# Low parts of the z weights, from the fifth block on, made by GpSimd instead of VectorE

## The chip, the cores and the metric

The program runs on one core of one Trainium2 chip. The metric is the device time of one execution in microseconds (us), taken as the median of three runs. The core has a matrix engine (TensorE, PE in the profile), a vector engine (VectorE, DVE), an activation engine (ScalarE, ACT), GpSimd (POOL) and a queue that issues DMAs (SyncE, SP).

## The reference

Three blocks of a network run over 256 tokens of width 1024, in float32. The stage that matters here belongs to the first of them, an RWKV-7 layer that has a convolution branch beside it. Cut to the lines that this stage computes:

```python
proj = h @ w_in[i]                                   # 1024 -> 7168
p_r, p_k, p_v, p_c, z_rwkv, z_conv = jnp.split(proj, splits, axis=-1)
y_rwkv = rwkv7_time_mix(h, p_r, p_k, p_v, ...)       # a recurrence over the tokens
c = u * jax.nn.sigmoid(gate)                         # u, gate = split(p_c)
c = causal_depthwise_conv(c, conv_dw, 31 taps) + dw_b
y_conv = jax.nn.silu(layer_norm(c, ln_w, ln_b)) @ w_o
merged = jax.nn.sigmoid(z_rwkv) * y_rwkv + jax.nn.sigmoid(z_conv) * y_conv
```

## The kernel before, in words

Every large matrix product is made of three products of split float32 values: `w_hi*x_hi + w_hi*x_lo + w_lo*x_hi`. A weight matrix arrives in units of 512 columns in one of two buffers `raw`. A unit is cut in four items of 128 columns. For each item ScalarE copies the raw weights to the rounded `w_hi[m]` (`act_head`, L498) and VectorE makes `w_lo[m] = raw - w_hi[m]`, 128 partitions by 1024 elements (`dve_rest`, L504). SyncE loads the next unit into a buffer half when the `w_lo_ready` count says that its two items have been used.

The layer `z` (the projections z_rwkv and z_conv) is 16 such items, j = 0 to 15, and is not done in a stretch of its own. TensorE spreads its blocks (L2349 to L2351, 24 products of 128x256 each) over the chunk loop of the recurrence. Two blocks come before the loop, and the eight chunks c = 0 to 7 have 2, 2, 2, 2, 1, 1, 1 and 3 blocks (`Z_CHUNK`). The item that block j + 4 will use is prepared once block j is done: ScalarE makes its high part in the same chunk (L1038 and L971), VectorE its low part one chunk later, between the evacuations of z blocks (L1648). Items 4 and 5 are prepared before the loop, in the middle of a triangular inverse that VectorE computes by substitution (L1580 and L1582).

One chunk passes between the engines in this order:

- TensorE: x products (L2435, L2439), eight transposes (L2244), the z blocks, y products (L2449), u products (L2457).
- VectorE and ScalarE: half of the u rows each (VectorE L1721, L1722; "u rows" below).
- VectorE: the state times its decay (L1733, two inputs in SBUF), the masks of the next chunk's products (L1679, two of them, which read PSUM), the state plus the new products (L1688, which reads PSUM). TensorE's x products of the next chunk wait for the masks and for the state.
- VectorE, behind that and in its program order: 12 or 16 taps of the convolution (L1670, 128 by about 240 elements, two inputs in SBUF), then the evacuations of the z blocks and the low parts.

VectorE's instructions are executed in order, so the u rows of a chunk wait for its taps, evacuations and low parts. GpSimd has nothing to do in the loop before chunk 6, where it issues two DMAs (L746).

Of the kernel before, what the change touches and what calls it, by code (L numbers as in the profile page):

```python
# [18 lines left out]
F32 = mybir.dt.float32  # L19
F32R = mybir.dt.float32r  # L20
ALU = mybir.AluOpType
# [3 lines left out]
P = 128  # L25
# [6 lines left out]
M_PER_UNIT = UNIT_COLS // P  # L32
# [47 lines left out]
def build(nc, a, out):  # L80
    ctx = ExitStack()
    with ctx:
        sems = {}

        def sem(name):
            if name not in sems:
                sems[name] = ctx.enter_context(nc.semaphore(name))
            return sems[name]
# [5 lines left out]
        raw = [sb(f"raw{i}", [P, KC, UNIT_COLS]) for i in range(2)]  # L94
        w_hi = [sb(f"w_hi{i}", [P, KC, P], F32R) for i in range(M_PER_UNIT)]
        w_lo = [sb(f"w_lo{i}", [P, KC, P], F32R) for i in range(M_PER_UNIT)]
# [53 lines left out]
        Z_EARLY, Z_CHUNK = 2, (2, 2, 2, 2, 1, 1, 1, 3)  # L150
# [153 lines left out]
        L = {}  # L304
# [32 lines left out]

        landed = [[0, 0], [0, 0]]
        unit, item, evac = 0, 0, 0
        occupant, kept_by_k = [[None, None], [None, None]], [False, False]  # L340
        for ly in order:
            ly.u0, ly.item0, ly.evac0 = unit, item, evac
            ly.landed, ly.free = ([], []), ([], [])
            for u in range(len(ly)):
                s = unit % 2
                for half in range(2):
                    landed[s][half] += 16 * ly.dmas[half]
                    ly.landed[half].append(landed[s][half])
                    ly.free[half].append(occupant[s][1 if ly.by_k != kept_by_k[s] else half])
                    occupant[s][half] = ("w_lo_ready", item + M_PER_UNIT // 2 * (half + 1))  # L350
                    if half:
                        kept_by_k[s] = ly.by_k
                unit += 1
                item += M_PER_UNIT
                if u % ly.k_split == ly.k_split - 1:
                    evac += M_PER_UNIT
            ly.item1, ly.evac1 = item, evac
# [18 lines left out]
        BANKS = M_PER_UNIT  # L376
# [123 lines left out]
        def dve_rest(dve, ly, u, p, m):  # L500
            s = (ly.u0 + p) % 2
            nk = ly.nkc[u] if isinstance(u, int) else KC
            dve.wait_ge(sem("w_hi_ready"), ly.item0 + M_PER_UNIT * u + m + 1)
            dve.tensor_tensor(piece(ly, u, w_lo[m], nk, m), raw_piece(ly, u, s, nk, m), piece(ly, u, w_hi[m], nk, m).bitcast(F32),  # L504
                              ALU.subtract).then_inc(sem("w_lo_ready"), 1)
# [116 lines left out]
        @block.sync  # L622
        def _(sp):
            sp.dma_start(x_tok, a["x"][0].rearrange("(c p) d -> p c d", p=P)).then_inc(sem("x_loaded"), 16)

            load_params(sp, range(1), "par_first", slice(0, PAR_SHARE))
            for ly in order:
                s0 = ly.u0 % 2
                def body(u, p, last):
                    s = (ly.u0 + p) % 2  # L630
                    nk = ly.nkc[u] if isinstance(u, int) else KC
                    for half in range(2):
                        parts = ly.sources(u)[half:half + 1] if ly.by_k else [x for x in ly.sources(u) if x[0].start // HALF == half]
                        if not parts:
                            continue

                        if not isinstance(u, int):
                            sp.wait_ge(sem("w_lo_ready"), ly.item0 + M_PER_UNIT * (u - 2) + M_PER_UNIT // 2 * (half + 1))
                        elif ly.free[half][u]:
                            sp.wait_ge(sem(ly.free[half][u][0]), ly.free[half][u][1])  # L640
                        for c, src in parts:
                            dst = raw[s][:, c, :] if ly.by_k else raw[s][:, 0:nk, c]
                            sp.dma_start(dst, src).then_inc(sem(f"landed{s}{half}"), 16)
                if ly.name == "down0":
                    sp.wait_ge(sem("w_lo_ready"), L["up0"].item1)
                    sp.dma_start(dt_w, a["ssd_w_in_2"][0].rearrange("(k p) n -> p k n", p=P)[:, :, 5120:5120 + SSD_HEADS]).then_inc(sem("dt_w_loaded"), 16)
                if ly.name == "down1":
                    sp.wait_ge(sem("w_lo_ready"), L["up1"].item1)
                    sp.dma_start(fox_w, a["fox_w_in_2"][0].rearrange("(k p) n -> p k n", p=P)[:, :, 4 * D:4 * D + FOX_HEADS]).then_inc(sem("small_loaded"), 16)
                if ly.name == "down2":  # L650
                    sp.dma_start(gain_last, a["final_norm_g_2"].rearrange("(a d) -> a d", a=1).broadcast_to([P, D])).then_inc(sem("small_loaded"), 16)
                if ly.name == "conv_out":
                    for i, name in enumerate(("ssd_dt_bias_2", "ssd_a_log_2")):
                        sp.dma_start(heads_col[:, i:i + 1], a[name][0].rearrange("(h a) -> h a", a=1)).then_inc(sem("small_loaded"), 16)
                    sp.dma_start(heads_col[0:FOX_HEADS, 2:3], a["fox_b_f_2"][0].rearrange("(h a) -> h a", a=1)).then_inc(sem("small_loaded"), 16)
                    for h in range(2):
                        for i, name in enumerate(("fox_q_norm_g_2", "fox_k_norm_g_2")):
                            sp.dma_start(fox_g[64 * h:64 * h + 64, i:i + 1], a[name][0].rearrange("(d a) -> d a", a=1)).then_inc(sem("small_loaded"), 16)
                        sp.dma_start(d_rows[64 * h:64 * h + 64, :], a["ssd_d_2"][0].rearrange("(a h) -> a h", a=1).broadcast_to([64, SSD_HEADS])).then_inc(sem("small_loaded"), 16)
                if ly is order[0]:  # L660
                    for u in range(len(ly)):
                        if u == 2:

                            load_params(sp, range(1, par_tiles), "par_loaded")
                        body(u, u % 2, False)
                    for i, (n, rows) in enumerate((("decay_w2", slice(0, 64)), ("a_2", slice(64, 128)), ("g_2", slice(0, 128)))):
                        sp.dma_start(w2[rows, D * i:D * i + D], a[n][0]).then_inc(sem("small_loaded"), 16)
                else:
                    units(sp, ly, body)
            for i in range(4):  # L670
                c, b = divmod(i, 2)
                half = slice(UNIT_COLS * b, UNIT_COLS * b + UNIT_COLS)
                sp.wait_ge(sem(f"y_tok_ready{b}"), c + 1)
                sp.dma_start(out[0, c * P:(c + 1) * P, half], y_tok[:, c, half]).then_inc(sem("out_done"), 16)
            sp.wait_ge(sem("out_done"), 64)
# [3 lines left out]
        def _(pool):  # L679
# [55 lines left out]
            for r in range(4):  # L735
                pool.dma_start(lt[quarter[r]], sub_in[quarter[r]].rearrange("s (y t) -> y s t", t=CHUNK)).then_inc(sem("sub_dma"), 16)

            pool.wait_ge(sem("dve_stages"), INVERSES_MADE)
            link(pool.memset(state, 0.0))
            pool.nop().then_inc(sem("pool_stages"), 1)  # L740

            pool.wait_ge(sem("bonus_out"), 16)
            pool.wait_ge(sem("ln_act"), 2)
# [674 lines left out]
        def _(dve):  # L1418
# [212 lines left out]
                    substitute(done, done + SUB_STEPS[i - SUB_BLOCK])  # L1631

            def z_rest(j):
                dve_rest(dve, L["z"], j // M_PER_UNIT, j // M_PER_UNIT % 2, j % M_PER_UNIT)

            def z_rests(first, last):
# [270 lines left out]
            ly = L["ssd_xbc"]  # L1907
# [192 lines left out]
            ly = L["fox_v"]  # L2100
# [113 lines left out]
        def _(pe):  # L2214
# [122 lines left out]
            def z_blocks(first, last, c=None):  # L2337

                ly = L["z"]
                for j in range(first, min(last, len(ly) * M_PER_UNIT)):  # L2340
                    m = j % M_PER_UNIT
                    if j % 2 and c is not None:
                        pe.wait_ge(sem("x_rows_a"), c + 1)
                    pe.wait_ge(sem("w_lo_ready"), ly.item0 + j + 1)
                    if j >= 2:

                        pe.wait_ge(sem("evac_done"), ly.evac0 + BANKS + j - 1)
                    for k in range(KC):
                        mm(z_bank(j), w_hi[m][:, k, :], x_hi[:, k, :], start=k == 0, stop=False)  # L2349
                        mm(z_bank(j), w_hi[m][:, k, :], x_lo[:, k, :], start=False, stop=False)  # L2350
                        ins = mm(z_bank(j), w_lo[m][:, k, :], x_hi[:, k, :], start=False, stop=k == KC - 1)  # L2351
                    ins.then_inc(sem("block_done"), 1)
# [409 lines left out]
```

## Time and profile before

| | us |
|---|---|
| median of three runs | 1379.92 |
| lowest and highest | 1376.66, 1382.22 |
| the profiled execution | 1387.18 |
| its span in the trace | 1385.4 |

The profiled execution is 7.3 us above the median. Its span is 1.8 us shorter than its own time. Time stamps of rows are in us from the start of the span. In a timeline row stand the start, the duration, the engine, the line, the operation with its output and inputs, how many instructions of one kind were merged, and in brackets the idle time of the engine before it and what ended it. A duration of one instruction includes the time from its start to its end on the engine, and two that follow each other overlap by about 0.1 us.

### The profile page before, as it was taken

The page shows a single profiled execution, that of the slowest core. Times are in us where ns is not written, and L with a number is a line of the kernel's source. Part 1 is how long each engine was busy: PE and PEld are TensorE (multiplying, and loading weights), DVE is VectorE, ACT ScalarE, POOL GpSimd, SP SyncE. Part 2 cuts the span into 40 slices and gives each one's busy share as a digit, 9 for nine tenths or more (in the row PEclk, how much of TensorE's full clock was granted, in tenths as well). Part 3 has the DMA queues.
Part 4 walks back from the last instruction along what each step waited for, and adds up shares of the span by engine and source line. Part 5 has one row for each costly group of instructions (what it writes and reads, how often), then busy time and mean ns, then how long its engine had stood idle before and what let it go on. Part 6 is the DMA issues. An engine that isn't in the chain of part 4 may idle for free.

```text
span 1385.4 us, 30051 instructions
## 1 busy us (share of the span) xinstructions
PE 1329.5 (96%) x12384; PEld 1267.8 (92%) x12384; DVE 992.7 (72%) x1636; ACT 774.7 (56%) x1353; POOL 116.5 (8%) x151
## 2 busy tenths in 40 slices
PE   5999999999999999999997999999999999999998
PEld 5998978989989999989995899999999888999986
DVE  4769898978876665575898868886565554877754
ACT  4596775549455443454669654444455554644443
POOL 2000100000002110000203001111000100122100
PEclk8999998999999999999999999999999998999999
DMA  7643620223545537645672355546664621555461
GB/s 226 195 140 123 191 86 27 70 68 118 183 153 183 183 122 232 189 132 182 199 213 75 121 175 164 183 150 208 190 183 166 196 65 57 188 183 182 163 212 66
DMA packets 197810, 212.70 MB, mean 154 GB/s; under 512 B 8972, under 2 KB 186924, under 8 KB 197564
## 3 DMA queue, kind: packets, MB, share of 16 engines
q1 hardware_dynamic: 195132, 201.46, 45.4%
q0 software_dynamic: 2464, 9.52, 2.3%
q8 instruction: 89, 1.46, 0.4%
q14 instruction: 29, 0.24, 0.1%
q10 hardware_dynamic: 96, 0.02, 0.0%
HBM read 209.33 MB, written 1.65 MB: 152 GB/s over the span
## 4 chain that ended last, share of the span: by engine, by line
PE 88%; DVE 6%; ACT 2%; SPq 2%; issue 1%; DMA 1%; DVEq 0%; ACTq 0%
PE pb L458 21%; PE pb L459 21%; PE pb L460 21%; PE pb L2405 2%; PE pb L2729 1%; PE pb L2730 1%; PE pb L2731 1%; PE pb L2244 1%; PE pb L2233 1%; SPq L610 1%; DVE w_lo L504 1%; PE pb L2349 1%; PE pb L2350 1%; PE pb L2351 1%; DVE pj L1670 1%
## 5 line engine op out<-in xcount | busy, mean ns | idle before, releaser
L504 DVE TENSOR_TENSOR w_lo<-raw,w_hi 128x1024 fp32r<-128x1024 f32 (+2 forms) x384 | 465.6, 1216 | 139.6 <-ACT w_hi L498 138.4
L498 ACT ACTIVATE w_hi<-raw 128x1024 fp32r<-128x1024 f32 (+2 forms) x384 | 396.6, 1041 | 301.1 <-PE pb L460 221.4
L458 PE MATMUL pb<-x_hi,w_hi 128*128 128x256 f32 x1856 | 529.6, 285 | 5.9 <-DVE x_lo L1427 3.5
L459 PE MATMUL pb<-x_lo,w_hi 128*128 128x256 f32 x1856 | 527.1, 284 | 0.0
L460 PE MATMUL pb<-x_hi,w_lo 128*128 128x256 f32 x1856 | 526.9, 284 | 0.0
L458 PEld LDWEIGHTS pb<-x_hi,w_hi 128*128 128x128 f32 x1856 | 358.2, 193 | 8.8 <-DVE w_lo L504 6.7
L459 PEld LDWEIGHTS pb<-x_lo,w_hi 128*128 128x128 f32 x1856 | 358.3, 193 | 0.2
L460 PEld LDWEIGHTS pb<-x_hi,w_lo 128*128 128x128 f32 x1856 | 358.2, 193 | 0.0
L753 POOL TENSOR_TENSOR sub<-sub,rstd 128x256 f32<-128x256 f32 x66 | 72.0, 1106 | 584.1 <-ACT sub L1146 584.1
L458 PE MATMUL pb<-act_hi,w_hi 128*128 128x256 f32 x392 | 111.1, 284 | 3.3 <-DVE w_lo L504 3.3
L460 PE MATMUL pb<-act_hi,w_lo 128*128 128x256 f32 x392 | 110.9, 283 | 0.0
L459 PE MATMUL pb<-act_lo,w_hi 128*128 128x256 f32 x352 | 99.6, 283 | 0.0
L1146 ACT ACTIVATE sub<-sub 128x256 f32<-128x256 f32 x66 | 26.5, 415 | 100.7 <-DVE sub L1875 84.0
L458 PEld LDWEIGHTS pb<-act_hi,w_hi 128*128 128x128 f32 x392 | 75.2, 192 | 3.7 <-DVE w_lo L504 3.7
L460 PEld LDWEIGHTS pb<-act_hi,w_lo 128*128 128x128 f32 x392 | 75.3, 192 | 0.0
L459 PEld LDWEIGHTS pb<-act_lo,w_hi 128*128 128x128 f32 x352 | 67.6, 192 | 0.0
L1846 DVE TENSOR_TENSOR sub<-pb,rstd 128x256 f32<-128x256 f32 x66 | 27.8, 423 | 45.3 <-PE pb L460 42.6
L1852 DVE TENSOR_TENSOR sub<-pb,sub 128x256 f32<-128x256 f32 x66 | 27.7, 420 | 40.1 <-PE pb L460 22.2
L1153 ACT ACTIVATE act_hi<-sub 128x256 f32 (+1 forms) x66 | 27.3, 416 | 45.5 <-DVE sub L1852 45.5
L1670 DVE SCALAR_TENSOR_TENSOR pj<-pj,par 128x255 f32<-128x255 f32 (+29 forms) x120 | 48.3, 464 | 0.9
L1444 DVE TENSOR_TENSOR pj<-pb,rstd 128x256 f32<-128x256 f32 x64 | 26.9, 422 | 25.3 <-PE pb L460 24.0
L2244 PE MATMUL pb<-ident,pj 128*128 128x128 f32 (+1 forms) x195 | 34.9, 323 | 9.4 <-DMA pj<-in_x_dram 6.0
(363 smaller groups left out, 2277.1 us busy)
## 6 DMA issues: line engine op xcount, KB each, us to landing
raw<-in_ffn_w_up_dram SPq DMA_DIRECT2D x55, 1024.0 KB, 5.1
raw<-in_w_in_dram SPq DMA_DIRECT2D x28, 1024.0 KB, 5.1
raw<-in_ssd_w_in_dram SPq DMA_DIRECT2D x20, 1024.0 KB, 5.3
raw<-in_ffn_w_down_dram SPq DMA_DIRECT2D x16, 1024.0 KB, 5.6
raw<-in_fox_w_in_dram SPq DMA_DIRECT2D x16, 1024.0 KB, 5.8
raw<-in_ffn_w_down_dram SPq DMA_DIRECT2D x16, 896.0 KB, 5.8
raw<-in_ffn_w_gate_dram SPq DMA_DIRECT2D x11, 1024.0 KB, 5.3
raw<-in_ssd_w_out_dram SPq DMA_DIRECT2D x8, 1024.0 KB, 5.2
```

The costliest lines, as they stand in the source:

```text
L458: pe.matmul(o, w_hi[m][:, k, :], hi[:, k0 + k, :], start=first and k == 0, stop=False)
L459: pe.matmul(o, w_hi[m][:, k, :], lo[:, k0 + k, :], start=False, stop=False)
L460: mm = pe.matmul(o, w_lo[m][:, k, :], hi[:, k0 + k, :], start=False, stop=final and k == nk - 1)
L498: act.activation(piece(ly, u, w_hi[m], nk, m), raw_piece(ly, u, s, nk, m), ACT.Copy).then_inc(sem("w_hi_ready"), 1)
L504: dve.tensor_tensor(piece(ly, u, w_lo[m], nk, m), raw_piece(ly, u, s, nk, m), piece(ly, u, w_hi[m], nk, m).bitcast(F32), ALU.subtract).the ...
L753: pool.tensor_tensor(s_tile[m], s_tile[m], rstd[:, :], ALU.mult).then_inc(sem("glu_silu"), 1)
L1153: act.activation(o, a_tile[m], ACT.Copy).then_inc(sem("act_hi_ready"), 1)
L1670: go(stt(o[:, s:T], c[:, 0:T - s], w, o[:, s:T], ALU.mult, ALU.add))
L1846: tt(g_tile[m], pb[m][:, 0:T], rstd[:, :], ALU.mult).then_inc(sem("evac_done"), 1)
L1852: tt(a_tile[m - 2], pb[m][:, 0:T], s_tile[m - 2], ALU.mult).then_inc(sem("evac_done"), 1)
L2244: return pe.transpose(o, i, ident[0:n, 0:n])
L2405: ins = mm(pb[PAIR_BANKS[q][a]][side[c], s:T], diag[(2 * i + c) % NDIAG][side[a], :], slot(U)[side[a], 2 * q + c, 0:T - s], start=s == 0, ...
```

## The change

GpSimd subtracts the high parts for items 4 to 15 of the layer `z`, in a new function `z_low` that waits for the high part (`w_hi_ready`) and counts in a semaphore of its own, `low_z`. It makes items 4 and 5 before it waits for the inverse (L739 before), and the other ten behind it, ahead of its two DMAs of the bonus term. Where VectorE made these 12 low parts there now stands a nop that only raises `w_lo_ready`. TensorE waits for `low_z` as well before z block j, and so does SyncE before it refills a half of `raw` that these items occupied.

```diff
+        POOL_LOW = {}
+        POOL_LOW["z"] = lambda u, last: M_PER_UNIT * (u - 1) + last
...
                             sp.wait_ge(sem(ly.free[half][u][0]), ly.free[half][u][1])
+                            if ly.free[half][u][3] > 0:
+                                sp.wait_ge(sem(f"low_{ly.free[half][u][2]}"), ly.free[half][u][3])
...
+            def z_low(j):
+
+                ly, m = L["z"], j % M_PER_UNIT
+                s = (ly.u0 + j // M_PER_UNIT) % 2
+                pool.wait_ge(sem("w_hi_ready"), ly.item0 + j + 1)
+                pool.tensor_tensor(w_lo[m][:, :, :], raw[s][:, :, P * m:P * m + P], w_hi[m][:, :, :].bitcast(F32),
+                                   ALU.subtract).then_inc(sem("low_z"), 1)
+            for j in range(BANKS, BANKS + Z_EARLY):
+                z_low(j)
             pool.wait_ge(sem("dve_stages"), INVERSES_MADE)
             link(pool.memset(state, 0.0))
             pool.nop().then_inc(sem("pool_stages"), 1)
+            for j in range(BANKS + Z_EARLY, len(L["z"]) * M_PER_UNIT):
+                z_low(j)
...
             def z_rest(j):
+                if j >= BANKS:
+
+                    dve.nop().then_inc(sem("w_lo_ready"), 1)
+                    return
                 dve_rest(dve, L["z"], j // M_PER_UNIT, j // M_PER_UNIT % 2, j % M_PER_UNIT)
...
                     pe.wait_ge(sem("w_lo_ready"), ly.item0 + j + 1)
+                    if j >= BANKS:
+                        pe.wait_ge(sem("low_z"), j - BANKS + 1)
```

VectorE at the end of chunk 1, before the change: the last taps, the two evacuations with the low parts of items 6 and 7, the u rows, the decayed state and the masks.

```order
L1670 SCALAR_TENSOR_TENSOR pj<-pj,par 128x242 x3
L1648 TENSOR_TENSOR pj<-pb,rstd 128x256 [waits block_done,dve_chain]
L504 TENSOR_TENSOR w_lo<-raw,w_hi 128x1024 [waits w_hi_ready]
L1648 TENSOR_TENSOR pj<-pb,rstd 128x256 [waits block_done]
L504 TENSOR_TENSOR w_lo<-raw,w_hi 128x1024 [waits w_hi_ready]
L1721 COPY pj<-pb 32x2x128 [waits u_done]
L1722 COPY pj<-pb 32x2x128
L1733 TENSOR_TENSOR sub<-sub,chunk_decay 128x512 [waits y1_done]
```

The same place after the change (lines of the changed kernel: L1668 is the evacuation, L1741 and L1742 the u rows, L1753 the decayed state).

```order
L1690 SCALAR_TENSOR_TENSOR pj<-pj,par 128x242 x3
L1668 TENSOR_TENSOR pj<-pb,rstd 128x256 [waits block_done,dve_chain]
L1668 TENSOR_TENSOR pj<-pb,rstd 128x256 [waits block_done]
L1741 COPY pj<-pb 32x2x128 [waits u_done]
L1742 COPY pj<-pb 32x2x128
L1753 TENSOR_TENSOR sub<-sub,chunk_decay 128x512 [waits y1_done]
```

The two subtractions have left VectorE's queue between the evacuations and the u rows; nothing else has moved.

GpSimd from its loads for the inverse to the DMAs of the bonus, before the change.

```order
L736 DMA sub<-sub_in 32x32x32 x3
L739 MEMSET sub 128x512 [waits dve_stages]
L746 DMA pj<-bonus_dram 64x8x256 [waits pool_chain,ln_act,bonus_out]
L746 DMA pj<-bonus_dram 64x8x256
```

The same place after the change (L748 is the subtraction in `z_low`, L753 the memset of the state, L762 the DMAs).

```order
L741 DMA sub<-sub_in 32x32x32 x3
L748 TENSOR_TENSOR w_lo<-raw,w_hi 128x1024 [waits w_hi_ready] x2
L753 MEMSET sub 128x512 [waits dve_stages]
L748 TENSOR_TENSOR w_lo<-raw,w_hi 128x1024 [waits pool_chain,w_hi_ready]
L748 TENSOR_TENSOR w_lo<-raw,w_hi 128x1024 [waits w_hi_ready] x9
L762 DMA pj<-bonus_dram 64x8x256 [waits ln_act,bonus_out]
```

Twelve subtractions now stand on GpSimd, two ahead of the memset and ten between it and the DMAs.

## Rows read from the trace of the kernel before

**Rows 1.** The page, busy time of each engine

```profile
PE 1329.5 (96%) x12384; PEld 1267.8 (92%) x12384; DVE 992.7 (72%) x1636; ACT 774.7 (56%) x1353; POOL 116.5 (8%) x151
```

**Rows 2.** Timeline of VectorE and TensorE: substitution, and its first user

```profile
189.26 2.36 DVE L504 TENSOR_TENSOR w_lo<-raw,w_hi 128x1024 fp32r<-128x1024 f32 x2
...
206.21 3.54 PE L2416 MATMUL pb<-ident,sub 32*32 32x32 f32 x233
```

**Rows 3.** Timeline of VectorE, early taps to the u rows of chunk 0

```profile
203.37 18.50 DVE L1670 SCALAR_TENSOR_TENSOR pj<-pj,par 128x255 f32<-128x255 f32 x44
...
222.76 0.42 DVE L1648 TENSOR_TENSOR pj<-pb,rstd 128x256 f32<-128x256 f32 x1 [0.44 <-PE pb L2351]
224.47 0.41 DVE L1721 COPY pj<-pb 32x256 f32<-32x256 f32 x1 [1.29 <-PE pb L2457]
```

**Rows 4.** Timeline of VectorE, chunks 1 and 2

```profile
239.75 0.69 DVE L1733 TENSOR_TENSOR sub<-sub,chunk_decay 128x512 f32<-128x512 f32 x1
...
242.60 6.52 DVE L1670 SCALAR_TENSOR_TENSOR pj<-pj,par 128x241 f32<-128x241 f32 x16
...
252.21 0.41 DVE L1721 COPY pj<-pb 32x256 f32<-32x256 f32 x1
...
253.10 0.69 DVE L1733 TENSOR_TENSOR sub<-sub,chunk_decay 128x512 f32<-128x512 f32 x1
```

**Rows 5.** Timeline of VectorE, chunks 4 and 5

```profile
276.95 2.35 DVE L504 TENSOR_TENSOR w_lo<-raw,w_hi 128x1024 fp32r<-128x1024 f32 x2
...
280.23 0.69 DVE L1733 TENSOR_TENSOR sub<-sub,chunk_decay 128x512 f32<-128x512 f32 x1
...
296.53 0.69 DVE L1688 TENSOR_TENSOR sub<-sub,pb 128x512 f32<-128x512 f32 x1 [2.48 <-PE pb L2478]
```

**Rows 6.** Timeline of TensorE, u products of chunks 2 and 4

```profile
250.91 0.69 PE L2457 MATMUL pb<-pj 32*32 32x64 f32 x32
...
276.28 0.69 PE L2457 MATMUL pb<-pj 32*32 32x64 f32 x32
```

**Rows 7.** Timeline of ScalarE, high parts of items 6, 7, 9, 10, 11, 14

```profile
219.94 1.06 ACT L498 ACTIVATE w_hi<-raw 128x1024 fp32r<-128x1024 f32 x1 [0.92 <-PE pb L2351]
222.76 1.06 ACT L498 ACTIVATE w_hi<-raw 128x1024 fp32r<-128x1024 f32 x1 [1.75 <-PE pb L2351]
...
237.14 1.06 ACT L498 ACTIVATE w_hi<-raw 128x1024 fp32r<-128x1024 f32 x1 [1.75 <-PE pb L2351]
...
247.26 1.05 ACT L498 ACTIVATE w_hi<-raw 128x1024 fp32r<-128x1024 f32 x1
249.97 1.06 ACT L498 ACTIVATE w_hi<-raw 128x1024 fp32r<-128x1024 f32 x1 [1.67 <-PE pb L2351]
...
275.49 1.04 ACT L498 ACTIVATE w_hi<-raw 128x1024 fp32r<-128x1024 f32 x1
```

**Rows 8.** Instructions of two lines of GpSimd: min/median/max ns

```profile
L753 POOL TENSOR_TENSOR sub<-sub,rstd x66: 727/752/1612, 419.7 to 1317.8; 128x256 f32<-128x256 f32 x66
L719 POOL TENSOR_TENSOR sub<-sub x3: 1269/1294/1525, 17.9 to 20.9; 128x512 f32<-128x512 f32 x3
```

**Rows 9.** Timelines of GpSimd and VectorE where the two meet

```profile
425.51 2.23 POOL L753 TENSOR_TENSOR sub<-sub,rstd 128x256 f32<-128x256 f32 x2 [4.33 <-ACT sub L1146]
...
436.08 1.20 POOL L753 TENSOR_TENSOR sub<-sub,rstd 128x256 f32<-128x256 f32 x1 [1.66 <-ACT sub L1146]
...
427.48 1.34 DVE L504 TENSOR_TENSOR w_lo<-raw,w_hi 128x1024 fp32r<-128x1024 f32 x1
...
435.47 1.22 DVE L504 TENSOR_TENSOR w_lo<-raw,w_hi 128x1024 fp32r<-128x1024 f32 x1
```

**Rows 10.** Eight transposes before the z blocks, chunks 2 and 3

```profile
243.12 1.06 PE L2244 MATMUL pb<-ident,pj 128*64 128x128 f32 x8
...
256.70 1.91 PE L2244 MATMUL pb<-ident,pj 128*64 128x128 f32 x8
```

**Rows 11.** Window of chunk 3: busy time per engine, clock, DMA share, GB/s

```profile
256.00:259.00 3.00, 2.93 (x44) 2.49 (x44) 2.96 (x9) 0.80 (x3) 0.00 (x0) 0.50 0.21 68
```

More of the change, by code:

```diff
@@ L349, in build @@
                     ly.free[half].append(occupant[s][1 if ly.by_k != kept_by_k[s] else half])
-                    occupant[s][half] = ("w_lo_ready", item + M_PER_UNIT // 2 * (half + 1))
+                    last = M_PER_UNIT // 2 * (half + 1)
+                    occupant[s][half] = ("w_lo_ready", item + last, ly.name, POOL_LOW[ly.name](u, last) if ly.name in POOL_LOW else 0)
                     if half:
```

## The prediction

> **What bounds the kernel now.** I read the busy times first [rows 1]: TensorE is busy for 96% of the span, VectorE for 72%, GpSimd for 8%. A change of VectorE's load therefore counts only where TensorE waits for VectorE. The chain that ended last, followed through the stretch from 175 to 330 us, passes to VectorE in one recurring place: at a chunk's end through the u rows, the decayed state L1733, the masks L1679 and the state sum L1688, and from there to TensorE's x products of the next chunk. So I read VectorE's timeline chunk by chunk and asked of every u-rows row whether VectorE had been idle before it. In chunk 0 it was idle for 1.29 us, and for 0.44 us one instruction earlier [rows 3]. In chunk 2 it was not: the u rows start at 252.21 [rows 4], but TensorE's products for them had ended at 250.91 + 0.69 = 251.60 [rows 6]. In chunk 4 TensorE was done at 276.97 [rows 6], and VectorE was still in two low parts from 276.95 on [rows 5]. Those two places are where the 12 subtractions cost time today.
>
> **What is removed.** Twelve subtractions, two in 2.36 us [rows 2], so 14.1 us of VectorE's work. Items 4 and 5 lie in the substitution, whose result TensorE first uses at 206.21 [rows 2], about six us after it is done: worth nothing by themselves. In chunks 1 and 3 VectorE waits for TensorE behind them, in chunks 5 and 6 TensorE's sums of the layer norm are the longer part (VectorE idles for 2.48 us before L1688 of chunk 5 [rows 5]): nothing either. Chunk 2 has 252.21 - 251.60 = 0.6 us to give, chunk 4 has 279.3 - 276.97 = 2.4 us (the low parts start at 276.95 and take 2.35 [rows 5]). The removal alone is worth 3.0 us.
>
> **What one subtraction takes on GpSimd.** Before, GpSimd has no operation of 128x1024. Its two-input operation on 256 elements takes 0.727 us at least and on 512 takes 1.269 us [rows 8], so 256 more elements cost 0.542 us. Going on by that step, 1024 elements take 1.269 + 2 x 0.542 = 2.35 us; four times the 256-element median of 0.752 us gives 3.0 us. I call the value p and take 2.35 us, because the step comes from the largest sizes that the trace has, and keep 2.35 and 3.0 as its bounds. A cheaper one I exclude: the two sizes show no gain per element that would bring it below. The page "GPSIMD Engine Reference" of the Trainium skill, section 3.1, gives 4497 ns for 2048 float32 elements; half of that is an estimate of 2.25 us, with which the sum below would be 3.6 instead of 4.2. No low part is late by this: item 6 is ready some 20 us before its block in chunk 2.
>
> **What it does to VectorE.** The trace shows the two engines in each other's way when both read two inputs from SBUF. GpSimd's instruction at 436.08 starts while VectorE's subtraction of 435.47 to 436.69 runs and takes 1.20 us instead of 0.75 [rows 8, 9]; it ends 0.59 us after VectorE does. The other way round, GpSimd's pair that starts at 425.51 ends at 427.74; VectorE's subtraction that starts at 427.48 takes 1.34 us instead of 1.22, and ends 1.08 us after GpSimd's end [rows 9]. The one that starts second seems to wait for the first. These overlaps of VectorE are short, 0.26 us at most, so that a stall over a whole GpSimd instruction isn't shown by rows, only extrapolated.
>
> The page "SBUF — State Buffer" of the Trainium skill, section "Who interferes with whom", states it as a rule: VectorE with two SBUF inputs and GpSimd reading SBUF share a read port, and the later one blocks fully until the first is done, while a VectorE instruction with one SBUF input doesn't contend. By that rule the sum is the 4.2 us below; without it, 3.0 us would be gained. The trace agrees as far as its short overlaps go.
>
> VectorE's instructions with two SBUF inputs are here the taps L1670 and the decayed state L1733. The evacuations, u rows, masks and the state sum take an operand from PSUM; that GpSimd doesn't hold them is an assumption. So I lay each subtraction at the end of its high part [rows 7] and ask what it meets:
>
> - Items 4 and 5, in the substitution: two stalls of at most 2 x 2.35 = 4.7 us against 2.36 us removed, with reductions of one input running underneath. VectorE ends between 0 and 2.3 us later; I take 0.4. TensorE has six us here, but the early taps, which end at 221.87 [rows 3], then end at about 222.2.
> - Chunk 0: item 6 asks at 219.94 + 1.06 = 221.00, gets in behind a tap at about 221.4 and holds until 223.75. Two taps of 0.4 us are left. One runs; item 7, which asks at 223.82, gets in at 224.15 and holds until 226.5. Then the last tap 0.4 and two evacuations 0.8: the u rows start at 221.4 + 2p + 1.6 = 227.7 instead of 224.47 [rows 3]. Cost 2p - 1.5 = **+3.2**.
> - Chunk 1: item 9 asks at 238.20 and holds until 240.55; L1733 is due at 239.75 [rows 4]. Cost p - 1.55 = **+0.8**. Item 8 meets only evacuations. Nothing hides the delay, as x products follow the masks at once.
> - Chunk 2: item 10 asks at 248.31, in the last taps, which end at 249.12 [rows 4]; with the stall they end at 251.45 and the evacuations at 252.25, where the u rows stood before (252.21). The 0.6 us that were to be gained are gone. Item 11 asks at 251.03, gets in at 251.4 and holds until 253.75; L1733 was at 253.10. Cost p - 1.7 = **+0.65**.
> - Chunk 3 repeats chunk 1, with the same distance of 1.55 us: **+0.8**.
> - Chunk 4: item 14 asks at 276.53, as the taps end, and holds until 278.95. The u rows, no longer held up, are done by 277.9, so L1733 starts at 278.95 instead of 280.23 [rows 5]. Cost p - 3.63 = **-1.3**.
> - Chunk 5: item 15 delays L1733 by half a us, under the 2.48 us that VectorE idles behind it. Nothing. The bonus DMAs on GpSimd's queue, now behind ten subtractions, go out at 309.75 us, long after item 15. Nothing. The extra nops and waits: under 0.1 us each, hidden with their engines' other work.
>
> The sum is 6p - 9.9, with p = 2.35 **+4.2 us**.
>
> One more term is TensorE's clock. In chunk 3 the granted clock is 0.50, the lower of its two levels (1.2 GHz), at the transposes and the first z products [rows 11]; the eight transposes take 1.91 us, against 1.06 in chunk 2 [rows 10], and with the products around them a chunk loses about 1.4 us. Before, chunks 1, 3 and 5 are hit and 2 and 4 not. The small products ahead of the transposes are stretched by the 0.8 us of chunks 1 and 3, which makes that more likely in 2 and 4. It would cost 1.1 us in chunk 2 and 1.3 in chunk 4, where the gain would go. I count half of both, **+1.2 us**.
>
> Together +5.4 us, on the profiled execution's 1387.18 us 1392.6 (span 1385.4 to 1390.8). That execution is above the median of the three runs, 1379.92 us, from which the forecast starts: **1385.3 us**.
>
> **The rivals.**
>
> - *The engines don't block each other for long.* VectorE would then merely lose its 12 subtractions: -3.0 us, 1377 us. For it: the trace has no long stall of VectorE by GpSimd. Against it: both rows above [rows 9], and that every overlap in them costs. Chance 0.13.
> - *A subtraction costs GpSimd 3.0 us or more* (its raw operand is eight pieces of 128 elements, which no operation before has). The sum is 6 x 3.0 - 9.9 = +8.1, with the clock's 1.2 +9.3: 1389.2 us. From p = 2.8 the sum alone is over 6.9 us, which is 0.5%. For it: items 6 and 7, which stall the taps of chunk 0, count twice. Against it: the step between the two sizes measured. A clock that falls in both chunks brings p = 2.35 to +6.6, just short of that bound. Chance of this side 0.28.
> - *The low part comes late and TensorE waits for `low_z`.* It would have to be late by 20 us; chance 0.02 or less, in which the time would be over 1390.
>
> **How the numbers follow.** The forecast, a stall of a few us in the loop, has 0.57. The range reaches from the first rival to past the second: 1376.5 to 1391 us; the likeliest case's own range is 1382 to 1388. Within 0.5% (6.9 us, about what a measurement of this kernel can tell from no change) lie the forecast and the first rival; the chances are 0.03 faster, 0.69 same, 0.28 slower.
>
> **What the changed profile would show.** GpSimd's 12 rows at 2.4 us where VectorE is in evacuations, and longer where it starts in a tap. Single taps, or L1733 of chunks 1 to 3, longer by up to 2.4 us, with the idle time gone. The u rows of chunk 0 some 3 us later, and L1733 of chunk 4 relatively earlier. If taps keep their 0.4 us while GpSimd works, the blocking is wrong and with it the sign. If GpSimd's rows are over 2.8 us outside of the taps, p is.

## The result and the profile after

The changed kernel takes 1393.74 us (median of six runs, 1388.46 to 1396.41), the kernel before 1380.77 us in the same six comparisons: ratio 1.0089, 95% interval 1.0069 to 1.0109, so about 12.3 us slower (9.5 to 15.1). The forecast was 1385.3 us with a range up to 1391.0: the direction was the likeliest case's, the size was not. Two runs stand outside of all means and ratios below, one of 1448.98 us of the kernel before, at a mean granted clock of 0.84, and one of 3255.26 us of experiment e11.

The page after, head and busy times (as in [rows 1]):

```profile
span 1391.4 us, 30074 instructions
PE 1329.5 (96%) x12384; PEld 1268.6 (91%) x12384; DVE 991.5 (71%) x1624; ACT 774.3 (56%) x1353; POOL 145.3 (10%) x163
```

VectorE has lost 12 instructions and only 1.2 us of busy time, where 14.1 us of work were taken away. The difference is in instructions that last longer. The 12 subtractions on GpSimd, with their least, median and greatest duration in ns:

```profile
L748 POOL TENSOR_TENSOR w_lo<-raw,w_hi x12: 2353/2383/3340, 181.4 to 300.6; 128x1024 fp32r<-128x1024 f32 x12
```

GpSimd's timeline (L748 is the subtraction):

```profile
181.39 5.67 POOL L748 TENSOR_TENSOR w_lo<-raw,w_hi 128x1024 fp32r<-128x1024 f32 x2 [34.63 <-ACT w_hi L501]
...
219.41 2.45 POOL L748 TENSOR_TENSOR w_lo<-raw,w_hi 128x1024 fp32r<-128x1024 f32 x1 [17.46 <-ACT w_hi L501]
222.22 2.51 POOL L748 TENSOR_TENSOR w_lo<-raw,w_hi 128x1024 fp32r<-128x1024 f32 x1 [0.36 <-ACT w_hi L501]
...
243.17 2.37 POOL L748 TENSOR_TENSOR w_lo<-raw,w_hi 128x1024 fp32r<-128x1024 f32 x1 [0.42 <-ACT w_hi L501]
...
284.11 2.44 POOL L748 TENSOR_TENSOR w_lo<-raw,w_hi 128x1024 fp32r<-128x1024 f32 x1 [8.48 <-ACT w_hi L501]
```

VectorE in the same stretches (L1596 substitution; L1635 the gated product; L1690 taps; L1741 u rows; L1753 decayed state):

```profile
182.44 2.39 DVE L1635 TENSOR_TENSOR pj<-pj 128x1024 f32<-128x1024 f32 x1
...
185.65 2.79 DVE L1596 TENSOR_TENSOR sub<-sub 128x768 f32<-128x768 f32 x1
...
195.91 1.52 DVE L1596 TENSOR_TENSOR sub<-sub 128x768 f32<-128x768 f32 x1
...
204.44 22.61 DVE L1690 SCALAR_TENSOR_TENSOR pj<-pj,par 128x255 f32<-128x255 f32 x44
...
227.88 0.41 DVE L1741 COPY pj<-pb 32x256 f32<-32x256 f32 x1
...
244.65 1.44 DVE L1753 TENSOR_TENSOR sub<-sub,chunk_decay 128x512 f32<-128x512 f32 x1
...
258.72 1.43 DVE L1753 TENSOR_TENSOR sub<-sub,chunk_decay 128x512 f32<-128x512 f32 x1
...
278.34 8.47 DVE L1690 SCALAR_TENSOR_TENSOR pj<-pj,par 128x233 f32<-128x233 f32 x16
...
287.30 0.41 DVE L1741 COPY pj<-pb 32x256 f32<-32x256 f32 x1
```

A substitution step of 768 elements takes 2.79 us beside GpSimd's subtraction and 1.52 us ten microseconds later, without it. The 44 early taps take 22.61 us instead of 18.50 [rows 3]; the decayed state of chunks 1 and 2 takes 1.44 and 1.43 us instead of 0.69 [rows 4]; the train of 16 taps in which GpSimd starts at 284.11 takes 8.47 us, and the two trains of 16 before it, undisturbed or nearly, take 6.46 and 6.51 us. TensorE waits for what comes behind:

```profile
228.79 1.97 PE L2500 MATMUL pb<-pj,sub 64*64 64x64 f32 x32 [5.00 <-DVE pj L1742]
230.56 1.86 PE L2504 MATMUL pb<-pj 64*64 64x32 f32 x32
...
288.22 1.97 PE L2500 MATMUL pb<-pj,sub 64*64 64x64 f32 x32 [2.68 <-DVE pj L1742]
```

The same batches in chunks 0 and 4 of the kernel before:

```profile
225.38 1.15 PE L2478 MATMUL pb<-pj,sub 64*64 64x64 f32 x32
226.37 1.07 PE L2482 MATMUL pb<-pj 64*64 64x32 f32 x32
...
280.25 1.15 PE L2478 MATMUL pb<-pj,sub 64*64 64x64 f32 x32 [2.20 <-DVE pj L1722]
```

So TensorE has five microseconds of idle time in chunk 0, where before there was none, and 2.68 in chunk 4, where there were 2.20. And the batches of small products are slower behind the wait: 1.97 and 1.86 us instead of 1.15 and 1.07. The windows with the granted clock (columns: the stretch, its length, PE, PEld, DVE, ACT and POOL busy, clock, DMA share, GB/s) show why:

```profile
228.00:240.00 12.00, 11.21 (x169) 10.52 (x170) 8.59 (x19) 4.59 (x14) 0.00 (x0) 0.64 0.01 3
291.00:301.00 10.00, 10.00 (x176) 9.09 (x174) 6.69 (x18) 3.42 (x7) 0.39 (x1) 0.65 0.04 13
321.50:328.50 7.00, 7.00 (x78) 6.86 (x58) 1.24 (x2) 6.70 (x14) 0.06 (x1) 0.53 0.67 152
```

A mean of 0.64 over 12 us is the lower level (1.2 GHz) for most of them; before, the stretches at the lower level, at the start of chunk 0 and in chunks 1, 3 and 5, are a few microseconds each [rows 11]. From the first x product of chunk 0 to the u products of chunk 7 the loop took 318.14 - 212.32 = 105.8 us before and 331.56 - 211.02 = 120.5 us after. By chunk, from one x product's start to the next (us; "filler" is the run e9 below, "delay" e10):

| chunk | 0 | 1 | 2 | 3 | 4 | 5 | 6 | 7 (to u) | sum |
|---|---|---|---|---|---|---|---|---|---|
| before | 15.22 | 14.40 | 13.35 | 15.07 | 12.05 | 15.29 | 12.44 | 8.00 | 105.8 |
| after | 21.33 | 15.22 | 14.07 | 16.15 | 13.99 | 16.35 | 12.44 | 10.99 | 120.5 |
| filler | 19.50 | 13.57 | 13.60 | 13.70 | 12.41 | 14.35 | 12.45 | 7.99 | 107.6 |
| delay | 23.61 | 14.81 | 13.35 | 15.16 | 13.44 | 16.35 | 12.45 | 10.97 | 120.1 |

The loop's 14.7 us are more than the spans' 6.0 us, because the profiled execution of the kernel before is 6 to 7 us slower than its median (part of it a stretch from 1148 to 1178 us with a mean clock of 0.83, against 1.00 in the one after); the medians, 13 us apart, fit the loop.

The whole loop as one window, first before, then after:

```profile
212.32:318.83 106.51, 102.71 (x2097) 94.75 (x2097) 86.62 (x171) 58.64 (x132) 1.38 (x2) 0.92 0.21 62
211.02:332.25 121.23, 110.45 (x2097) 102.24 (x2097) 86.76 (x166) 60.30 (x136) 25.46 (x12) 0.85 0.19 55
```

TensorE is idle for 10.8 us instead of 3.8, and busy for 7.7 us longer with the same 2097 products. In these two executions the loss is thus about half waiting and half the lower clock (36 us at the lower level instead of 17).

### The profile page after: what moved, and what is told of

Same layout as the page of the kernel before. It is cut to its first block, busy times and chain, and to the rows that moved or that the text cites. A ratio compares the mean times of both kernels' runs of the same rounds, so it can differ in the third digit from the quotient of the medians.

```text
span 1391.4 us, 30074 instructions
## 1 busy us (share of the span) xinstructions
PE 1329.5 (96%) x12384; PEld 1268.6 (91%) x12384; DVE 991.5 (71%) x1624; ACT 774.3 (56%) x1353; POOL 145.3 (10%) x163
## 4 chain that ended last, share of the span: by engine, by line
PE 80%; DVE 11%; ACT 3%; DMA 2%; SPq 2%; issue 2%; POOL 0%; DVEq 0%; ACTq 0%; POOLq 0%
PE pb L461 20%; PE pb L463 19%; PE pb L462 19%; DVE pj L1690 2%; DVE w_lo L507 2%; PE pb L2752 1%; PE pb L2753 1%; PE pb L2751 1%; PE pb L2253 1%; SPq L613 1%; PE pb L2264 1%; PE pb L2371 1%; PE pb L2372 1%; PE pb L2373 1%; ACT pj L1298 1%
## 5 line engine op out<-in xcount | busy, mean ns | idle before, releaser
L507 DVE TENSOR_TENSOR w_lo<-raw,w_hi 128x1024 fp32r<-128x1024 f32 (+1 forms) x372 | 451.2, 1216 | 139.6 <-ACT w_hi L501 138.7
L1690 DVE SCALAR_TENSOR_TENSOR pj<-pj,par 128x255 f32<-128x255 f32 (+29 forms) x120 | 54.5, 516 | 0.9
```

Of the source, the lines that this page charges most:

```text
L1690: go(stt(o[:, s:T], c[:, 0:T - s], w, o[:, s:T], ALU.mult, ALU.add))
```

## The experiments

Each kernel was timed beside the kernel before, and every ratio is to that one. "Loop" is the sum of the table above (105.8 us before), taken from the profiled execution.

### e1, the removal alone

```diff
+        POOL_ITEMS = ()
+        POOL_LOW["z"] = lambda u, last: sum(j < M_PER_UNIT * u + last for j in POOL_ITEMS)
...
-            for j in range(BANKS + Z_EARLY, len(L["z"]) * M_PER_UNIT):
+            for j in [j for j in POOL_ITEMS if j >= BANKS + Z_EARLY]:
                 z_low(j)
...
             def z_rest(j):
                 if j >= BANKS:
-
+                    dve.wait_ge(sem("w_hi_ready"), L["z"].item0 + j + 1)
                     dve.nop().then_inc(sem("w_lo_ready"), 1)
```

(The list of items on GpSimd is empty here. The loop for items 4 and 5 and TensorE's wait for `low_z` go by the same list.)

> The 12 low parts are left out altogether (w_lo of items 4 to 15 holds older values), VectorE only waits for the high part and raises the count, GpSimd does nothing for them. This is the removal without its replacement. Theory A (GpSimd's subtractions block VectorE through SBUF, everything else is a consequence): 3.0 us faster than before, the chunk loop (first x product of chunk 0 to the last y product of chunk 7, 109.5 us before, 124.2 after the change) at 106 to 108 us, a ratio near 0.998. Rival B (the loss comes from VectorE's altered order or from the clock that falls when VectorE runs ahead of TensorE, not from GpSimd): as slow as the changed kernel, ratio 1.005 to 1.010, loop over 118 us.

Measured: ratio 0.9996 (0.9979 to 1.0013). Rival B, an effect of VectorE's order alone, is out: nothing is lost. But the 3.0 us of gain don't show either (the interval just reaches 0.998). In the profiled execution the loop is 108.0 us; by the expectation's own measure, which reaches to the last y product, it is 111.7 us against 109.5 before, where 106 to 108 were expected. The gain is where it was forecast, chunk 4 takes 9.77 us instead of 12.05, but chunks 2 and 3 take 16.74 and 18.07 instead of 13.35 and 15.07. There TensorE stops twice in the middle of a batch of small products, at places where no engine released it:

```profile
242.11 0.47 PE L2462 MATMUL pb<-sub,pj 64*32 64x64 f32 x15 [1.15 <-issue]
...
258.66 0.65 PE L2458 MATMUL pb<-pj 32*32 32x64 f32 x11 [1.52 <-issue]
```

The window behind the first, with the clock in the third column from the right:

```profile
242.00:248.00 6.00, 5.89 (x42) 5.44 (x43) 4.89 (x13) 3.54 (x12) 0.00 (x0) 0.52 0.02 4
```

TensorE is at the lower clock there. What VectorE gives back in this execution, TensorE loses in gaps and clock. Over all 12 runs, though, the time at the lower clock is the same as before (41 us in both), so the clock isn't shown to be what takes the gain in the mean. Why the gaps are there and not in the kernel before wasn't found.

### e2, GpSimd writes but doesn't read

On top of e1:

```diff
+            pool.wait_ge(sem("inverse_rows"), CHUNK // INV_GROUP)
+            for j in range(BANKS + Z_EARLY, len(L["z"]) * M_PER_UNIT):
+                pool.wait_ge(sem("w_hi_ready"), L["z"].item0 + j + 1)
+                link(pool.memset(flat_sub[:, 1024:2048], 0.0))
+                link(pool.memset(flat_sub[:, 1024:2048], 0.0))
+                link(pool.memset(flat_sub[:, 1024:1536], 0.0))
```

> As the one before, the 12 low parts left out, but GpSimd runs three memsets (1024, 1024 and 512 elements, some 2.5 us in all) into unused memory at each of the ten places behind the inverse where the changed kernel subtracts (items 6 to 15). They write and read nothing. Theory A in the form that only GpSimd instructions that read SBUF hold VectorE's second operand: VectorE's taps and decayed states keep their 0.4 and 0.69 us, time as without the memsets, ratio 0.996 to 1.000. If any GpSimd instruction holds VectorE: taps stalled as after the change, ratio 1.005 or more. Rival B as for the run without memsets.

Measured: 0.9994 (0.9977 to 1.0012). GpSimd and VectorE in chunk 0:

```profile
224.15 0.95 POOL L760 MEMSET sub<- 128x1024 f32 x1
...
224.57 0.69 DVE L1758 TENSOR_TENSOR sub<-sub,chunk_decay 128x512 f32<-128x512 f32 x1
```

The decayed state runs wholly inside a memset and keeps its 0.69 us. It does so in chunks 1 to 3 too, where it runs beside two memsets each. GpSimd being busy and writing SBUF at the same places isn't what holds VectorE. That its reads are is what is left; no run has an instruction that only reads.

### e3, the two items that should meet nothing

```diff
+        POOL_ITEMS = (8, 12)
...
             def z_rest(j):
-                if j >= BANKS:
+                if j in POOL_ITEMS:
```

and likewise in `z_low`'s loops, in TensorE's wait and in SyncE's counts. The next four experiments differ in this tuple alone.

> GpSimd makes the low parts of items 8 and 12 only; VectorE makes the ten others as before. By the model of stalls those two begin behind the taps of chunks 1 and 3 and end before the decayed state, so they meet no two-input instruction, and their removal shortens VectorE's way to the u rows of chunk 2 by 0.6 us and of chunk 4 by 1.2 us. Theory A: 1.8 us faster than before, ratio 0.997 to 1.001. Rival B (any hand-over to GpSimd costs 1 us an item): 2 us slower, ratio over 1.001.

Measured: 0.9993 (0.9970 to 1.0015), loop 105.0 us. The expected gain of 1.8 us is too small to be told from nothing, and the interval doesn't quite exclude the rival either. In the trace the decayed state has 0.69 us in all chunks. But item 12 does meet something: it starts 0.75 us before the train of taps in chunk 3 would have ended, holds it for 2.1 us (8.57 instead of 6.45), and TensorE gets a wait that the kernel before hasn't:

```profile
255.36 8.57 DVE L1691 SCALAR_TENSOR_TENSOR pj<-pj,par 128x237 f32<-128x237 f32 x16
...
261.06 2.61 POOL L749 TENSOR_TENSOR w_lo<-raw,w_hi 128x1024 fp32r<-128x1024 f32 x1 [23.40 <-ACT w_hi L502]
...
267.94 1.23 PE L2501 MATMUL pb<-pj,sub 64*64 64x64 f32 x32 [1.47 <-DVE pj L1743]
```

In return the wait of 2.20 us in chunk 4 is gone altogether. Item 12 met nothing in the changed kernel (the train of chunk 3 has 6.46 us there): whether an item collides depends on the rest of the loop.

### e4, e5, e6, e7: which items cost

> GpSimd makes items 4 to 7 only, the ones that meet the substitution and the early taps; VectorE makes items 8 to 15 as before. Theory A: this carries the loss of chunk 0, which in the profile of the changed kernel is 6.1 of the 14.7 us by which the loop grew; so 5 to 6 us slower than before, ratio 1.003 to 1.005, with u rows of chunk 0 some 3 to 5 us late and the clock down behind them. If the loss is spread over the loop in proportion to the items (4 of 12): 4.3 us, ratio 1.003, without a stall of over 2 us in chunk 0.

> GpSimd makes items 6 and 7 only, whose two subtractions meet the last early taps of chunk 0; 4 and 5 stay with VectorE, so the substitution is not held. Theory A: the taps end about 4.7 us later than their own length allows (two subtractions of 2.4 us), minus 1 us that the substitution no longer loses; the u rows of chunk 0 come 2 to 4 us late, the whole is 3 to 6 us slower than before, ratio 1.002 to 1.004. Rival C (the substitution's hold by items 4 and 5 is what makes chunk 0 late): no loss, ratio under 1.001.

> GpSimd makes items 4, 5 and 8 to 15; VectorE makes 6 and 7 as before. Theory A: chunk 0 is as before (item 4 and 5 cost the substitution 1 us, of which TensorE waits nothing), and what is left is the decayed state held in chunks 1, 2 and 3 (+0.8, +0.7, +0.8) and item 14 in the taps of chunk 4 (0 to +1.9): 2 to 4 us slower than before, ratio 1.001 to 1.003, and the first wait of TensorE for u rows is short (before: none). Rival (the loss is made by the ten late items together): ratio over 1.005.

> GpSimd makes only the three items whose subtraction meets the decayed state (9, 11, 13). Theory A: the row of the decayed state is 1.4 us instead of 0.69 in chunks 1, 2 and 3, +0.7 us each, against which one low part less stands before the u rows of chunk 2 (-0.6) and of chunk 4 (-1.2): 0 to 1 us slower, ratio 1.000 to 1.002, and no tap longer than 0.5 us.

| items on GpSimd | ratio (95% interval) | loop, us | TensorE's wait in chunk 0, us |
|---|---|---|---|
| 4 to 7 | 1.0063 (1.0044 to 1.0081) | 116.5 | 5.23 |
| 6, 7 | 1.0048 (1.0029 to 1.0068) | 114.0 | 3.94 |
| 4, 5, 8 to 15 | 1.0038 (1.0016 to 1.0060) | 114.1 | 0.52 |
| 9, 11, 13 | 1.0007 (0.9983 to 1.0031) | 107.9 | none |
| all twelve | 1.0089 (1.0069 to 1.0109) | 120.5 | 5.00 |

Items 4 to 7 cost 8.7 us, more than the 5 to 6 expected (their profiled execution is 8 us above their median). Two items of twelve, 6 and 7, make 6.6 us of the 12.3, somewhat more than the 3 to 6 expected. The rest makes 5.2 us, more than the 2 to 4 us expected; the rival's 1.005 lies inside the interval. The two ratios add up to the whole (0.0048 + 0.0038 = 0.0086), each known to about 3 us. In the third kernel the wait in chunk 0 is short, and yet the loop is at a mean clock of 0.87, against 0.92 before: a long wait in chunk 0 isn't needed for the clock to fall more often. Items 9, 11 and 13 hold the decayed state as forecast, in the kernel with these three alone:

```profile
237.44 1.72 DVE L1754 TENSOR_TENSOR sub<-sub,chunk_decay 128x512 f32<-128x512 f32 x1
252.62 1.43 DVE L1754 TENSOR_TENSOR sub<-sub,chunk_decay 128x512 f32<-128x512 f32 x1
268.30 1.42 DVE L1754 TENSOR_TENSOR sub<-sub,chunk_decay 128x512 f32<-128x512 f32 x1
```

and cost 1.0 us (-2.3 to +4.3), since each also removes a low part. Items 4 and 5 alone weren't run; by difference of the first two rows of the table they cost 2 us beside 6 and 7, less than the intervals can resolve.

### e8 and e9, the changed kernel with its idle time filled

```diff
                 else:
                     z_blocks(Z_FIRST[c] + 2, Z_FIRST[c + 1], c)
+                for _ in range({0: 36, 4: 18}.get(c, 0)):
+                    mm(pb[7][:, T:2 * T], x_hi[:, 0, 0:P], x_hi[:, 0, :], start=False, stop=False, skip_group_check=True)
```

(e8 had `start=True, stop=True`; that also changed the y sums, which are added up in the other half of the bank. e9 leaves them alone.)

> The changed kernel, with TensorE given products whose result nobody reads (36 of 128x256 in chunk 0 and 18 in chunk 4, 0.12 us each at full clock, into an unused half of a PSUM bank) just before it waits for the u rows, where it stands idle for 5.0 and 2.7 us in the changed kernel. If the idle time lets the granted clock fall and the lower clock behind it is part of the loss: the clock stays at 1.00 through chunk 1, the products behind the wait take 1.15 and 1.07 us instead of 1.97 and 1.86, and the kernel is 3 to 5 us faster than the changed one: ratio to before 1.005 to 1.007 instead of 1.009. If the clock plays no part: 1.009 as without the filler, or above.

> The changed kernel with the same idle-time products on TensorE as in the run before (36 in chunk 0, 18 in chunk 4), but added onto what stands in the unused half of the bank instead of starting a new sum there, because the first form also disturbed the y sums in the other half of that bank. Theory A (stalls of VectorE some 6 us, lower clock behind them some 8 us): the same time as with the first filler, ratio 1.002 to 1.004, loop from the first x product to the last u product 107 to 109 us (120.5 in the changed kernel, 105.8 before), no low-clock stretch behind chunk 0. Rival (the first filler was fast because the y values it left were different): ratio 1.007 to 1.009.

Measured: 1.0031 (1.0010 to 1.0051) and 1.0048 (1.0030 to 1.0067); the loop of the profiled execution is 107.6 us in both. The first is faster than the 1.005 to 1.007 expected, the second just slower than its 1.002 to 1.004, and both intervals exclude the 1.009 of no effect. All GpSimd subtractions are still there, and VectorE is held for no less in sum, though partly elsewhere: the 44 early taps take 22.63 us in e9, the trains of chunks 2 and 3 are held now and that of chunk 4 no longer:

```profile
244.68 8.66 DVE L1690 SCALAR_TENSOR_TENSOR pj<-pj,par 128x241 f32<-128x241 f32 x16
...
258.28 8.59 DVE L1690 SCALAR_TENSOR_TENSOR pj<-pj,par 128x237 f32<-128x237 f32 x16
...
271.87 6.39 DVE L1690 SCALAR_TENSOR_TENSOR pj<-pj,par 128x233 f32<-128x233 f32 x16
```

TensorE in chunk 0 of e9:

```profile
222.97 4.58 PE L2487 MATMUL pb<-x_hi 128*128 128x256 f32 x36
228.28 1.15 PE L2502 MATMUL pb<-pj,sub 64*64 64x64 f32 x32 [0.73 <-DVE pj L1742]
229.26 1.07 PE L2506 MATMUL pb<-pj 64*64 64x32 f32 x32
```

The window of e9 that answers to 228 to 240 us above:

```profile
222.00:234.00 12.00, 11.04 (x217) 10.43 (x218) 11.55 (x23) 3.92 (x11) 1.83 (x1) 1.00 0.01 3
```

Needless work on the busiest engine makes the kernel faster, by the difference of 1.0089 and the mean of the two, 1.0040, that is 6.8 us, give or take 3.4 by the intervals: about half of the loss was TensorE running at its lower clock behind a wait for VectorE. The rival of e9, that the first filler's y values mattered, is out, as its 1.007 lies above the interval. Both profiled executions are the fastest of their kernels (1379.10 and 1378.68 us, medians 1385.40 and 1387.38), with 14 to 17 us at the lower clock where the mean is 35 and 39. So the row "filler" above shows the loop at its best, not in the mean.

### e10, VectorE late without GpSimd

```diff
             conv_taps(0, DVE_EARLY)
+            dve.wait_ge(sem("inverse_rows"), CHUNK // INV_GROUP)
+            for _ in range(6):
+                link(tt(flat_sub[:, 1024:2048], flat_sub[:, 1024:2048], flat_sub[:, 1024:2048], ALU.subtract))
```

> The kernel before, with nothing on GpSimd, in which VectorE does six needless subtractions of 128x1024 (1.22 us each, 7 us in all) in dead memory at the end of the early taps. By the slack of 1.7 us there the u rows of chunk 0 come 5.2 us late, as in the changed kernel, and no later chunk is touched. Theory A (a long wait costs its length and then the lower clock behind it): TensorE waits 5 us and low-clock stretches follow in chunk 1; the loop grows by 7 to 10 us, ratio 1.005 to 1.008. Rival D (the lower clock in the changed kernel comes from the later collisions, not from the wait in chunk 0): the loop grows by 5.2 us, ratio 1.004.

Measured: 1.0068 (1.0048 to 1.0088). VectorE is held for 7.5 us and TensorE waits longer than planned (timelines of VectorE and TensorE):

```profile
222.21 7.52 DVE L1696 TENSOR_TENSOR sub<-sub 128x1024 f32<-128x1024 f32 x6
...
231.47 1.97 PE L2481 MATMUL pb<-pj,sub 64*64 64x64 f32 x32 [7.93 <-DVE pj L1725]
233.23 1.86 PE L2485 MATMUL pb<-pj 64*64 64x32 f32 x32
```

The window of e10 behind it:

```profile
231.00:243.00 12.00, 11.53 (x169) 10.84 (x170) 8.63 (x19) 4.59 (x14) 0.00 (x0) 0.62 0.01 3
```

The wait came out longer than the 5.2 us expected: the u rows are ready 6.1 us later than before, and TensorE's products ahead of them were done 1.9 us earlier in this execution. The ratio alone doesn't separate theory A from rival D, since the wait of 7.9 us by itself would be 1.0057, inside the interval. The trace does: rows and clock behind the wait are those of the changed kernel (1.97 and 1.86 us, 0.62), and in the loop TensorE is busy for 109.5 us instead of 102.7 with the same products. In the table above its chunks 5 and 7 are as long as the changed kernel's to 0.02 us, with no GpSimd instruction in them. So the longer chunks 5 and 7 after the change aren't collisions. Chunk 7 begins at 320.6 us in both and falls to the lower clock; what decides that, the runs don't show.

### e11 and e12, filler where it might pay

Kernel before with 18 such products in its wait in chunk 4, and items 8 and 12 on GpSimd with 12 of them.

> The kernel before with 18 needless products of 128x256 on TensorE in its wait of 2.2 us in chunk 4, added onto an unused half bank. If the clock is worth having: the low-clock stretch of chunk 5 (283.0 to 287.0) is gone, 1 to 2 us faster than before, ratio 0.998 to 1.000; if not, the same time, or 0.3 us slower as the products outlast the wait.

> GpSimd makes items 8 and 12 only, and TensorE does 12 needless products in its wait of 1.5 us in chunk 4, where the run with items 8 and 12 alone has 6.8 us at the lower clock behind it. Theory A: the gains of both, loop 102 to 104 us instead of 105.8, 2 to 4 us faster than before, ratio 0.997 to 0.999. If the clock's fall there was chance: ratio as for items 8 and 12 alone, 0.999.

Measured: 0.9983 (0.9965 to 1.0001) and 0.9989 (0.9970 to 1.0007). Chunk 5 shrinks as expected, 13.81 us instead of 15.29 in the first (13.63 in the second). The whole may be 2 us faster in the first, which its interval just doesn't separate from nothing. In the profiled execution of the second, two other chunks (1 and 3) were longer (15.95 and 16.30 us) and the loop 109.0 us. Neither beats the kernel before clearly. The second is no test of its idea: the wait of 1.5 us that it was to fill stands in chunk 3 of e3, not in chunk 4. In chunk 4 TensorE had no wait, and its 12 products (1.70 us) only made the chunk longer, 13.12 us instead of e3's 11.92. Chunk 3 is long because item 12 starts at 263.15, inside the train of taps, which takes 8.57 us as in e3.

### Time at the lower clock, over all runs

Each run's mean granted clock gives its time at the lower level, 2 x (1 - clock) x time. The means over runs:

| kernel | runs | mean us | at the lower clock, us |
|---|---|---|---|
| before (three series) | 29, 26, 27 | 1380.8, 1382.5, 1381.3 | 41, 45, 41 |
| after | 6 | 1393.3 | 57 |
| e8, e9 (after, filled) | 12, 11 | 1386.0, 1386.8 | 35, 39 |
| e10 (VectorE late) | 6 | 1390.8 | 52 |
| e4, e5, e6 | 7, 7, 8 | 1390.6, 1390.0, 1388.4 | 54, 54, 52 |

The series stand beside e1 to e4, e5 to e8 and e9 to e12. Among the runs of the kernel before, a run with 1 us more at the lower clock is 0.34, 0.23 and 0.33 us longer in the three series, and in the other kernels 0.23 to 0.47. The change adds 16 us at the lower clock, worth some 5.5 us at 0.34 (4 to 7.5 by the other figures). That leaves 7 us for the waits.

## Why the prediction was wrong

- **What a subtraction takes, 2.35 us: right.** Twelve rows have 2.353 us at least and 2.383 in the middle. The rival of 3.0 us fell. The Trainium skill's "GPSIMD Engine Reference", section 3.1, by which I estimated 2.25 us, is within 6% of the trace.
- **The stall over the whole instruction: right, shown.** The decayed state goes from 0.69 to 1.44 us, the substitution step from 1.52 to 2.79 and the train of 16 taps from 6.39 to 8.47, which is 2.08 of the 2.44 us of item 14. e2 shows that writes alone don't do it. It agrees with the rule on the shared read port in the Trainium skill's "SBUF — State Buffer", "Who interferes with whom".
- **Chunk 0, +3.2 us: the place was right, the term too small.** The taps were to end at 226.9 and end at 227.05, the u rows were to start at 227.7 and start at 227.88. That both agree so closely is in part luck: the train began 1.07 us later than before, where 0.4 was taken, and was held for 4.11 us, where the sum has 4.7, two whole subtractions. And the sum took TensorE's side from one execution. In this one TensorE entered chunk 0 at 211.02 instead of 212.32, and the 1.3 us that it was early are lost in the wait. Of the chunk's +6.1 us, 3.4 are the later u rows, 1.3 this early start and 1.4 the slower products behind the wait; with the clock held up (e9) the chunk still costs +4.3 us.
- **Chunks 1 to 3, +0.8, +0.65, +0.8: right.** The decayed state lasts 0.74 us longer in each, and the chunks grew by 0.82, 0.72 and 1.08 us, together 2.6 against 2.25, with some of the clock's change in it. One step inside is wrong without an effect on the sum: item 10 was to hold the last taps of chunk 2, but starts 0.24 us before their end, when no further tap is due (6.51 us, before 6.52).
- **Chunk 4, -1.3 us: wrong.** It became +1.9 us, of which 0.5 are TensorE's longer wait (2.68 against 2.20) and most of the rest the slower products behind it. I put item 14's start, 276.53, at the end of the taps, 276.57, and took that for safe. Once the decayed state of chunk 3 ends later, the taps start later against TensorE, and item 14 starts 2.7 us before the end of the train (284.11 in 278.34 to 286.81): the collision that I had seen in chunk 0. VectorE then holds the u rows until 287.30, and the gain is gone. How thin the margin is shows in e9: there item 14 starts 0.3 us before the end of the train and holds no tap. (e9's chunk 4, +0.4 us, is therefore no price of the collision; its 18 needless products end 2.2 us after the u rows are ready.)
- **TensorE's clock, +1.2 us: the step that failed.** I took the 0.8 us by which chunks 1 and 3 grow for the only cause, and the lower clock in chunks 2 and 4 for the only price, 1.1 and 1.3 us, halved. I did not ask what a wait of 3 us and more in chunk 0, which the sum itself forecast, would do to the clock, although the prediction's own rows showed two levels in the loop. In the profiled executions TensorE is busy for 7.7 us longer in the loop with the same products; filling the waits takes 6.8 us away, give or take 3.4 (e8, e9); a wait without any collision brings the low stretches back (e10); and the time at the lower clock over all runs gives 5.5 us. So the term is 5.5 to 7.7 us, each estimate uncertain by some microseconds. Not all of it is the wait of chunk 0: e6, which has nearly none, also runs its loop at a lower mean clock.
- **The removal alone, 3.0 us: not confirmed.** e1 has 0.6 us (-1.8 to +2.9). The forecast gain in chunk 4 is there (2.3 us); two stops of TensorE and the clock take it back in chunks 2 and 3 of its profiled execution.

In sum: 5.5 to 7 us of waits where 4.2 were forecast, and about as much of lower clock where 1.2 were. The rival of a slower kernel had the right side with the wrong mechanism, a dearer subtraction.

## What to carry to other kernels

An instruction moved to GpSimd that reads SBUF isn't off VectorE where VectorE has two operands in SBUF: it can hold VectorE for nearly its whole length, here up to 2.1 of 2.4 us for 1.2 us saved, so count each one against the VectorE instruction that runs when it starts, with a margin, because every earlier stall moves the next one: items 10, 12 and 14 each collided in one kernel and not in another. Give a new wait of TensorE of several microseconds a term for the clock behind it as well. With waits of 3.9, 5.2 and 7.9 us in chunk 0 (e5, e4, e10) the kernel lost 6.6, 8.7 and 9.4 us, each to about 2.7, so the term reached from 1.5 to 3.5 us beyond the wait there, and more in the changed kernel with its several waits. Where such a wait can't be avoided, needless products into unused PSUM are worth a try; in the kernel before, with its one wait of 2.2 us, they brought no clear gain (e11).

## What the runs showed that I had not expected

- That 54 needless products on TensorE, the first 36 of them 4.58 us long, made the changed kernel 6.8 us faster, give or take 3.4.
- TensorE stops in the middle of a batch of 32 small products with nothing to wait for, for 1.15 and 1.52 us in e1 and 1.01 and 1.37 us in e2, after the same instruction of the same batch in chunks 2 and 3. The changed kernel has stops of 0.26 and 0.72 us in these chunks, the kernel before none in the loop. What holds the issue there stays open.
- With VectorE's train of taps running, a waiting GpSimd instruction gets in after one tap: its rows of 2.45 and 2.51 us are only 0.1 to 0.16 us over the 2.35 us that it takes undisturbed.
